# A hybrid Hyena, attention and mixture-of-experts block: inverse square roots by GpSimd as a power, in place of ScalarE's Sqrt and VectorE's reciprocal

## Chip, core and metric

The kernel runs on one core of a Trainium2 chip. The metric is device microseconds of one execution; a kernel is timed several times and the median counts. Before the change it is 795.36 us (three runs, 794.49 to 795.76).

## What is computed

One encoder block over 512 tokens of width 1024, in float32: a Hyena mixer (long convolutions by FFT) and grouped-query attention side by side, a cross-attention over 256 memory rows, and a mixture of 16 experts with two chosen per token. What matters here are its root-mean-square norms, which stand ahead of and behind every stage:

```python
def rms_norm(x, g):
    y = xf * lax.rsqrt(jnp.mean(xf * xf, axis=-1, keepdims=True) + EPS)
    return y * g

h = rms_norm(x, norm_mix)                      # 512 rows of 1024
q = rope_2d(rms_norm(q, q_norm), row, col)     # per head of 64; the same for k
y = concat(group_rms_norm(y_hyena, ...), group_rms_norm(y_attn, ...))   # groups of 64
x = x + y @ w_out
x = x + memory_cross_attn(rms_norm(x, norm_xattn), rms_norm(mem, norm_mem), ...)  # q, k normed per head of 128
x = x + hier_moe(rms_norm(x, norm_moe), ...)
```

## The kernel before

The tokens lie as four tiles of 128 partitions. Every engine has its own instruction stream, written out by hand, and the streams meet in semaphores; an engine works its stream strictly in order, so a wait holds everything behind it. A product with float32 accuracy is made of three TensorE products on split operands: ScalarE makes the high part (`weight_hi`, `split_hi`), VectorE the remainder (`weight_lo`, `split_lo`).

The streams run through these stages: filter spectra of the Hyena mixer with the norms of input and memory (0 to 75 us), its projections and transforms (to 205), the q, k, v projections with rope (to 258), the attention loop of 32 steps (8 heads by 4 tiles, to 345), the output projection (to 390), cross-attention (to 437), the router (to 492), then the experts in a loop of turns of 17.8 us each, bound by TensorE.

In the attention loop step `s` of each engine runs a little ahead of or behind the others. VectorE takes the score maximum of step s+3 (`gqa_max`) and the low part of the transposed probabilities of step s (`gqa_lo`); ScalarE takes the high part of step s and the exponential of step s+2 (`gqa_pt_hi`, `gqa_exp`), and every fourth step copies a finished head out of PSUM (`out_copy`, later `out_rows`); TensorE makes scores, transposes and, every second step, the head's product (`pv`), which needs the low parts of its two steps. GpSimd has little: it squares each head's output (`out_square`, L591), after ScalarE's `out_rows` of that head, in order of the heads, and from the router on it issues the stores, gathers and scatters of rows.

An inverse root takes three steps before: a sum of squares (ScalarE with an accumulator, or VectorE), ScalarE's Sqrt with scale and bias in one instruction (L691, L718, L872, L918, L960), and VectorE's reciprocal (L1188, L1192, L1445, L1458, L1463, L1521, L1581, L1592, L1602, L1658). Sqrt, Sin, Exp and Silu lie in different function tables of ScalarE, and a switch shows in the trace as an `ACT_TABLE_LOAD` on the line of the first function that needs it. Two dummy activations before (L883, L985) bring Exp's table in early, one (L943) brings Sqrt's.

Where the roots stand in order: input rows (L1187) and memory rows (L1191); memory keys (`head_rms(40, ...)`, L825, used at L1580); attention keys (L849, L1444); queries (L882, L1457); Hyena output (`hyena_root`, after step 13 of ScalarE, and `hyena_inverse`, in step 14 of VectorE); attention output in two parts (`out_root`, `out_normed`: six heads at step 29 and 30, two after the loop); the cross-attention norm (L1591), its queries (L984, L1601), and the four tiles ahead of the router (`tile_norm`, `tile_xn`).

Of the kernel before, what the change touches and what calls it, by code (L numbers as in the profile page):

```python
# [130 lines left out]
def build(nc, a, out, xn_dram, y_dram):  # L131
    with ExitStack() as ctx:
# [206 lines left out]
        s_rms = sem("rms_ready")  # L339
        s_ms = sem("head_sums_ready")  # L340
        s_hrms = sem("head_rms_ready")
# [9 lines left out]
        s_hroot = sem("hyena_root_ready")  # L351
        s_hrec = sem("hyena_inverse_ready")
        s_hwide = sem("hyena_inverse_wide")
        s_qinv = sem("qk_norms_ready")
# [222 lines left out]
        def _(pool):  # L577
# [9 lines left out]
            pool.memset(a2[FF:P, 0:1], 0.0).then_inc(s_w3, 1)  # L587

            pool.wait_ge(s_qinv, 1)
# [8 lines left out]
            for h in range(NQ):  # L598
                out_square(h)

            for i in range(TT):
                pool.wait_ge(s_xn, TT + 2 + i + 1)
                pool.dma_start(xn_dram[i * P:(i + 1) * P, :], xn[:, i, :]).then_inc(s_store, 16)
# [64 lines left out]
        def _(act):  # L668
# [16 lines left out]
            def rms(src, first, n, count):  # L685

                for i in range(n):
                    act.activation(fb_flat, src[:, i, :], ACT.Square, accum_out=small[:, first + i:first + i + 1])\
                        .then_inc(s_sq, 1)
                    act.wait_ge(s_sq, count - n + i + 1)  # L690
                act.activation(small[:, 16 + first:16 + first + n], small[:, first:first + n], ACT.Sqrt,  # L691
                               bias=eps, scale=1.0 / D).then_inc(s_rms, 1)
# [21 lines left out]

            def head_rms(first, n, width, count, floor=None):

                act.wait_ge(s_ms, count)
                act.activation(small[:, first:first + n], small[:, first:first + n], ACT.Sqrt, bias=eps if floor is None else floor,  # L718
                               scale=1.0 / width).then_inc(s_hrms, 1)
# [65 lines left out]
            act.activation(a2[FF:P, 1:T], mlp_arg[:, 1:T], ACT.Sin).then_inc(s_sin, 1)  # L785
            act.wait_ge(s_xn, TT + 1)
# [38 lines left out]
            head_rms(40, MT * MH, MHD, 1)  # L825
# [23 lines left out]
            head_rms(230, TT * NKV, HD, 2)  # L849
# [19 lines left out]
            def hyena_root():  # L869
                for n in range(len(HN_STEPS)):  # L870
                    wait_freed(act, ("hn", n))
                act.activation(small[:, 280:312], small[:, 280:312], ACT.Sqrt, bias=eps, scale=1.0 / HD).then_inc(s_hroot, 1)  # L872

            def inverse_wide(c):
                act.wait_ge(s_hrec, 1)
# [6 lines left out]
            head_rms(240, TT * NQ, HD, 3)  # L882
            act.activation(small[:, 398:399], eps, ACT.Exp)  # L883
# [30 lines left out]
            def out_root(lo, hi, count):  # L914

                top = small[:, 340:340 + TT * NQ].rearrange("p (i h) -> p i h", h=NQ)[:, :, lo:hi]
                act.wait_ge(s_ms, count)
                act.activation(top, top, ACT.Sqrt, scale=1.0 / HD).then_inc(s_hrms, 1)  # L918

            for s in range(AHEAD):  # L920
                gqa_exp(s)
            for s in range(NSEQ):
# [13 lines left out]
                if s == HN_STEPS[-1] + 1:  # L936
                    hyena_root()
# [16 lines left out]
            def tile_norm(first, jobkey, count, i):  # L954
# [5 lines left out]
                act.activation(small[:, 16 + first + i:17 + first + i], small[:, first + i:first + i + 1], ACT.Sqrt,  # L960
                               bias=eps, scale=1.0 / D).then_inc(s_rms, 1)
# [22 lines left out]
            head_rms(40, TT * MH, MHD, 6)  # L984
            act.activation(small[:, 398:399], eps, ACT.Exp)  # L985
# [52 lines left out]
            act.activation(rt[:, 204:208], rt[:, 200:204], ACT.Exp).then_inc(s_r4, 1)  # L1038

# [95 lines left out]
        def _(dve):  # L1135
# [37 lines left out]

            range_reduce(0)
# [16 lines left out]
            dve.wait_ge(s_rms, 2)  # L1191
            dve.reciprocal(small[:, 16:18], small[:, 16:18]).then_inc(s_xn, 1)  # L1192
# [251 lines left out]
            dve.wait_ge(s_hrms, 2)  # L1444
            link(dve.reciprocal(small[:, 230:238], small[:, 230:238]))  # L1445
# [63 lines left out]
            def out_roots(lo, hi):  # L1509
# [5 lines left out]
                dve.scalar_tensor_tensor(top, bottom, EPS * HD, top, ALU.mult, ALU.add).then_inc(s_ms, 1)  # L1515

            def out_normed(lo, hi, roots):
# [9 lines left out]
            dve.wait_ge(s_qinv, 1)  # L1527
# [5 lines left out]
            for s in range(NSEQ):  # L1533
# [17 lines left out]
                if s == EARLY_STEP + 1:  # L1551
                    out_normed(0, EARLY, 4)
# [4 lines left out]
            out_normed(EARLY, NQ, 5)  # L1557
# [22 lines left out]
            dve.wait_ge(s_hrms, 1)  # L1580
            link(dve.reciprocal(small[:, 40:48], small[:, 40:48]))  # L1581
# [9 lines left out]
            dve.wait_ge(s_rms, 2 + TT)  # L1591
# [967 lines left out]
```

## Time and profile before

| | |
|---|---|
| median of three runs | 795.36 us |
| lowest, highest | 794.49, 795.76 us |
| span of the profiled execution, first to last instruction | 791.7 us |
| mean granted TensorE clock | 0.987 |
| TensorE busy (matmul) | 747.9 us, 94% |
| VectorE busy | 603.7 us, 76% |
| ScalarE busy | 461.6 us, 58% |
| GpSimd busy | 78.0 us, 10% |

The profile is of one execution; its time outside the span is not on the page, so its span stands beside the runs' median, 3.7 us above it. A busy share is an average over stages with different limits: whether an engine's time counts is read from the chain of work that ended last, which goes back from the last instruction, at each step to what released it.

In the rows below a timeline line gives the start in us, the duration, the engine and line, what was written and read, and in brackets the idle time before it with what ended that; a line of the chain gives start, duration and the work, without what hides behind it. GpSimd is called POOL, TensorE PE, VectorE DVE, ScalarE ACT.

### The profile page before, as it was taken

What the parts mean: (1) busy time and instruction counts of PE and PEld (TensorE: products, weight loads), DVE (VectorE), ACT (ScalarE), POOL (GpSimd) and SP (SyncE); (2) the same over time, 40 slices, a digit from 0 to 9 for tenths busy, and PEclk for the clock granted to TensorE, in tenths of its full rate; (3) what the DMA queues carried; (4) which work ended last, traced back from release to release, by engine and by line L of the source; (5) the groups of instructions that cost most, each with busy time, mean ns of one, the idle gap of its engine ahead of it and who ended that gap; (6) DMA issues with size and microseconds to landing.
All of it is one profiled execution on the core that took longest, in us unless ns stands there. A gap on an engine that the chain in (4) does not pass through costs nothing.

```text
span 791.7 us, 10886 instructions
## 1 busy us (share of the span) xinstructions
PE 747.9 (94%) x3680; PEld 607.8 (77%) x3680; DVE 603.7 (76%) x930; ACT 461.6 (58%) x689; POOL 78.0 (10%) x94
## 2 busy tenths in 40 slices
PE   5899999999999898889999999999999999999994
PEld 3664858788898787678787787888888888888882
DVE  5767482997799877835548568899899999999882
ACT  5952333131233988621559333787888888887782
POOL 0000000000000000000000001122222232222111
PEclk9999999999999999999999998999999999999997
DMA  8830203020120200022130675999999999999741
GB/s 291 298 107 1 84 23 106 27 80 1 38 96 27 78 31 1 2 62 97 54 116 18 246 294 182 420 364 385 379 372 383 373 391 372 369 369 383 306 159 21
DMA packets 28542, 146.53 MB, mean 185 GB/s; under 512 B 4791, under 2 KB 6711, under 8 KB 21976
## 3 DMA queue, kind: packets, MB, share of 16 engines
q1 hardware_dynamic: 23320, 135.53, 45.3%
q0 software_dynamic: 5184, 10.50, 5.0%
q8 instruction: 23, 0.38, 0.2%
q14 instruction: 15, 0.12, 0.0%
HBM read 141.81 MB, written 12.58 MB: 195 GB/s over the span
## 4 chain that ended last, share of the span: by engine, by line
PE 72%; DVE 15%; ACT 6%; DMA 4%; issue 3%; SPq 0%; POOL 0%; DVEq 0%; ACTq 0%; POOLq 0%
PE bank L1992 17%; PE bank L2378 11%; PE bank L2380 10%; PE bank L2379 10%; PE bank L1930 9%; PE bank L1937 3%; DMA slot<-in_w_down 2%; PE bank L2373 2%; PE bank L2004 1%; ACT w_hi L727 1%; PE bank L2292 1%; PE bank L2290 1%; PE bank L2291 1%; DVE w_lo L1165 1%; PE bank L2415 1%
## 5 line engine op out<-in xcount | busy, mean ns | idle before, releaser
L1849 DVE TENSOR_TENSOR e_lo<-slot,e_hi 128x1024 fp32r<-128x1024 f32 x192 | 221.4, 1218 | 9.4 <-ACT e_hi L1045 9.3
L1045 ACT ACTIVATE e_hi<-slot 128x1024 fp32r<-128x1024 f32 x192 | 188.2, 1061 | 7.7 <-DMA slot<-in_w_down 4.9
L1165 DVE TENSOR_TENSOR w_lo<-w_raw,w_hi 128x1024 fp32r<-128x1024 f32 x41 | 49.4, 1222 | 69.8 <-ACT w_hi L727 69.6
L727 ACT ACTIVATE w_hi<-w_raw 128x1024 fp32r<-128x1024 f32 x41 | 42.7, 1057 | 96.9 <-DMA w_raw<-in_w_in 63.2
L2378 PE MATMUL bank<-e_hi,hgT_hi 128*128 128x512 f32 x240 | 95.0, 396 | 0.3 <-DVE hgT_lo L1861 0.3
L2380 PE MATMUL bank<-e_hi,hgT_lo 128*128 128x512 f32 x240 | 93.6, 390 | 0.0
L2379 PE MATMUL bank<-e_lo,hgT_hi 128*128 128x512 f32 x240 | 93.4, 389 | 0.0
L2378 PEld LDWEIGHTS bank<-e_hi,hgT_hi 128*128 128x128 f32 x240 | 45.2, 189 | 9.5 <-DVE hgT_lo L1861 0.7
L2380 PEld LDWEIGHTS bank<-e_hi,hgT_lo 128*128 128x128 f32 x240 | 45.1, 188 | 9.6
L2379 PEld LDWEIGHTS bank<-e_lo,hgT_hi 128*128 128x128 f32 x240 | 45.1, 188 | 8.9
L2378 PE MATMUL bank<-e_hi,gaT_hi 128*128 128x512 f32 x120 | 48.1, 401 | 0.0
L2380 PE MATMUL bank<-e_hi,gaT_lo 128*128 128x512 f32 x120 | 46.9, 391 | 0.0
L2379 PE MATMUL bank<-e_lo,gaT_hi 128*128 128x512 f32 x120 | 46.8, 390 | 0.0
L1992 PE MATMUL bank<-hT_hi,w_hi 128*128 128x512 f32 x96 | 37.9, 395 | 0.0
L1992 PE MATMUL bank<-hT_lo,w_hi 128*128 128x512 f32 x96 | 37.4, 389 | 0.0
L1992 PE MATMUL bank<-hT_hi,w_lo 128*128 128x512 f32 x96 | 37.4, 389 | 0.0
L1992 PE MATMUL bank<-w_hi,hT_hi 128*128 128x512 f32 (+1 forms) x96 | 34.0, 354 | 0.8 <-DVE hT_lo L1171 0.8
L1992 PE MATMUL bank<-w_hi,hT_lo 128*128 128x512 f32 (+1 forms) x96 | 34.0, 354 | 0.0
L1992 PE MATMUL bank<-w_lo,hT_hi 128*128 128x512 f32 (+1 forms) x96 | 34.0, 354 | 0.0
L1063 ACT ACTIVATE hgT_hi<-bank 128x512 fp32r<-128x512 f32 x28 | 15.2, 596 | 31.1 <-PE bank L2373 31.1
L636 POOL DMA_INDIRECT out_dram<-eo,meta_i x16 | 25.4, 1588 | 76.7 <-ACT eo L1080 46.4
L1937 PE MATMUL bank<-ident,pr 128*128 128x128 f32 x160 | 24.8, 277 | 8.1 <-ACT pr L891 6.3
(395 smaller groups left out, 1671.6 us busy)
## 6 DMA issues: line engine op xcount, KB each, us to landing
slot<-in_w_down SPq DMA_DIRECT2D x16, 2048.0 KB, 16.6
slot<-in_w_gate SPq DMA_DIRECT2D x16, 2048.0 KB, 14.6
slot<-in_w_up SPq DMA_DIRECT2D x16, 2048.0 KB, 16.0
w_raw<-in_w_in SPq DMA_DIRECT2D x18, 512.0 KB, 3.5
w_raw<-in_w_out SPq DMA_DIRECT2D x8, 512.0 KB, 3.7
w_raw<-in_w_k_mem SPq DMA_DIRECT2D x4, 512.0 KB, 6.1
x_in<-in_x SPq DMA_DIRECT2D x4, 512.0 KB, 9.2
w_raw<-in_w_v_mem SPq DMA_DIRECT2D x4, 512.0 KB, 6.0
```

Source lines behind the costliest of these rows:

```text
L636: pool.indirect_dma_start(out[0], bass.IndirectOffsetOnAxis(ap=meta_i[:, q, 0:1], axis=0), eo[q][:], None, bounds_check=T - 1, oob_is_err= ...
L727: act.activation(w_hi[ring(m)][:], w_raw[ring(m)][:], ACT.Copy).then_inc(s_wh, 1)
L1045: act.activation(e_hi[buffer(b, j)][:], slot[slot_][:, 1024 * part:1024 * (part + 1)], ACT.Copy).then_inc(s_ehi, 1)
L1165: dve.tensor_tensor(w_lo[slot_][:], w_raw[slot_][:], w_hi[slot_][:].bitcast(F32), ALU.subtract)\
L1849: dve.tensor_tensor(e_lo[slot_][:, at_], slot[slot_][:, at_], e_hi[buffer(b, j)][:].bitcast(F32), ALU.subtract)\
L1930: ins = pe.matmul(dst, l, r, start=(n == 0), stop=(n == len(pairs) - 1))
L1937: ins = pe.transpose(bank(job)[:, n * width:(n + 1) * width], s, ident[:])
L1992: ins = pe.matmul(bank(job)[:, 0:width], left, right, start=(k == 0 and m == 0), stop=(final and m == 2))
L2373: ins = pe.transpose(banks[half][:, k * P:(k + 1) * P], hg[q][:, c:D:KT], ident[:])
L2378: pe.matmul(dst, act_hi, w_hi_, start=first, stop=False)
L2379: pe.matmul(dst, act_hi, w_lo_, start=False, stop=False)
L2380: return pe.matmul(dst, act_lo, w_hi_, start=False, stop=last)
```

## The change

Sqrt leaves ScalarE and reciprocal leaves VectorE. In their place VectorE makes the mean plus epsilon in one step (`tensor_scalar`, multiply and add), counts up `s_mean`, and waits for `s_root`; GpSimd waits for `s_mean`, raises the values to the power -1/2 in place and counts up `s_root`. GpSimd takes the fourteen roots in a fixed order within its own stream. The mean and the wait stand on VectorE where the reciprocal stood (for memory keys: at L1580). Exp's table is brought in by one dummy behind the second Sin, and Silu's by one behind the router's last Exp. The dummies L883, L943 and L985 go.

```diff
@@ gpsimd
-            pool.wait_ge(s_qinv, 1)
+            pool.wait_ge(s_w3, 1)
+            minus_half = small[:, 396:397]
+            link(pool.memset(minus_half, -0.5))
+            roots = [0]
+            def inverse_root(x):
+                roots[0] += 1
+                pool.wait_ge(s_mean, roots[0])
+                pool.tensor_tensor(x, x, minus_half.to_broadcast([P, x.shape[1]]), ALU.pow).then_inc(s_root, 1)
+            def out_inverse_root(lo, hi):
+                roots[0] += 1
+                pool.wait_ge(s_mean, roots[0])
+                x = small[:, 340:340 + TT * NQ].rearrange("p (i h) -> p i h", h=NQ)[:, :, lo:hi]
+                pool.tensor_tensor(x, x, minus_half.unsqueeze(2).to_broadcast([P, TT, hi - lo]), ALU.pow).then_inc(s_root, 1)
+            inverse_root(small[:, 20:24])
+            inverse_root(small[:, 16:18])
+            inverse_root(small[:, 230:238])
+            inverse_root(small[:, 240:272])
             pool.tensor_tensor(ident_pair[:], ident[:, 0:HD], ident[:, HD:P], ALU.add).then_inc(s_pair, 1)
...
             for h in range(NQ):
+                if h == 3:
+                    inverse_root(small[:, 280:312])
                 out_square(h)
-
+                if h == EARLY - 1:
+                    out_inverse_root(0, EARLY)
+            out_inverse_root(EARLY, NQ)
+            inverse_root(small[:, 40:48])
+            inverse_root(small[:, 24:28])
+            inverse_root(small[:, 40:56])
             for i in range(TT):
+                inverse_root(small[:, 28 + i:29 + i])
                 pool.wait_ge(s_xn, TT + 2 + i + 1)
                 pool.dma_start(xn_dram[i * P:(i + 1) * P, :], xn[:, i, :]).then_inc(s_store, 16)
@@ scalar
-                act.activation(small[:, 16 + first:16 + first + n], small[:, first:first + n], ACT.Sqrt,
-                               bias=eps, scale=1.0 / D).then_inc(s_rms, 1)
...
             act.activation(a2[FF:P, 1:T], mlp_arg[:, 1:T], ACT.Sin).then_inc(s_sin, 1)
+            act.activation(small[:, 398:399], eps, ACT.Exp)
...
-            head_rms(240, TT * NQ, HD, 3)
-            act.activation(small[:, 398:399], eps, ACT.Exp)
...
-                if s == HN_STEPS[-1] + 1:
-                    hyena_root()
...
-                if s == EARLY_STEP:
-                    act.activation(small[:, 398:399], eps, ACT.Sqrt)
-                    out_root(0, EARLY, 4)
...
-            out_root(EARLY, NQ, 5)
...
-            head_rms(40, TT * MH, MHD, 6)
-            act.activation(small[:, 398:399], eps, ACT.Exp)
...
             act.activation(rt[:, 204:208], rt[:, 200:204], ACT.Exp).then_inc(s_r4, 1)
+            act.activation(small[:, 398:399], eps, ACT.Silu)
@@ vector
+            roots = [0]
+            def inverse_root(dst, total, width, least=EPS):
+                roots[0] += 1
+                dve.tensor_scalar(dst, total, 1.0 / width, least, ALU.mult, ALU.add).then_inc(s_mean, 1)
+                dve.wait_ge(s_root, roots[0])
...
-            dve.wait_ge(s_rms, 1)
-            link(dve.reciprocal(small[:, 20:24], small[:, 20:24]))
+            dve.wait_ge(s_sq, TT)
+            inverse_root(small[:, 20:24], small[:, 4:8], D)
...
-            dve.wait_ge(s_hrms, 2)
-            link(dve.reciprocal(small[:, 230:238], small[:, 230:238]))
+            inverse_root(small[:, 230:238], small[:, 230:238], HD)
...
-            dve.wait_ge(s_hrms, 3)
-            dve.reciprocal(small[:, 240:272], small[:, 240:272]).then_inc(s_qinv, 1)
+            dve.wait_ge(s_ms, 3)
+            inverse_root(small[:, 240:272], small[:, 240:272], HD)
...
             def hyena_inverse():
-                dve.wait_ge(s_hroot, 1)
-                dve.reciprocal(small[:, 280:312], small[:, 280:312]).then_inc(s_hrec, 1)
+                for n in range(len(HN_STEPS)):
+                    wait_freed(dve, ("hn", n))
+                inverse_root(small[:, 280:312], small[:, 280:312], HD)
...
-                dve.wait_ge(s_hrms, roots)
-                link(dve.reciprocal(top, top))
+                inverse_root(top, top, HD, 0.0)
...
-            dve.wait_ge(s_hrms, 6)
-            link(dve.reciprocal(small[:, 40:56], small[:, 40:56]))
+            dve.wait_ge(s_ms, 4)
+            inverse_root(small[:, 40:56], small[:, 40:56], MHD)
...
             def tile_xn(i):
-                dve.wait_ge(s_rms, 2 + TT + i + 1)
-                link(dve.reciprocal(small[:, 28 + i:29 + i], small[:, 28 + i:29 + i]))
+                dve.wait_ge(s_sq, 6 + TT + i + 1)
+                inverse_root(small[:, 28 + i:29 + i], small[:, 12 + i:13 + i], D)
```

## Rows read from the trace of the kernel before

**Rows 1.** The page, chain that ended last: shares of the span by engine

```profile
PE 72%; DVE 15%; ACT 6%; DMA 4%; issue 3%; SPq 0%; POOL 0%; DVEq 0%; ACTq 0%; POOLq 0%
```

**Rows 2.** Groups by line, ACT: first and last of 13 table loads (us, ns | idle)

```profile
L695 ACT ACT_TABLE_LOAD x1 | 1.3, 1283 | 0.7 <-PEq L2550 0.7
...
L1070 ACT ACT_TABLE_LOAD x1 | 1.3, 1283 | 0.0
```

**Rows 3.** POOL: group by line; timeline at 259 us; one line, ns min/median/max

```profile
L596 POOL TENSOR_TENSOR o_sq<-att 128x256 f32<-128x256 f32 x8 | 5.3, 668 | 81.1 <-ACT att L912 81.1
...
258.99 0.32 POOL L590 TENSOR_TENSOR ident_pair<-ident 128x64 f32<-128x64 f32 x1 [258.16 <-DVE small L1458]
...
L624 POOL COPY gather_i<-rec_i x12: 734/740/1836, 527.6 to 722.8; 128x1 int32 x12
```

**Rows 4.** Timeline, DVE, at the key norm

```profile
244.74 0.20 DVE L1445 RECIPROCAL small<-small 128x8 f32<-128x8 f32 x1
244.97 0.69 DVE L1411 TENSOR_TENSOR qkv<-qkv,small 128x512 f32<-128x512 f32 x1
```

**Rows 5.** Timeline, DVE, at the query norm

```profile
258.55 0.35 DVE L1458 RECIPROCAL small<-small 128x32 f32<-128x32 f32 x1
...
258.94 0.69 DVE L1491 TENSOR_REDUCE small<-bank 128x1 f32<-128x512 f32 x1
```

**Rows 6.** Timeline, 23 to 42 us, then two pieces of the chain

```profile
23.79 0.18 DVE L1188 RECIPROCAL small<-small 128x4 f32<-128x4 f32 x1 [1.16 <-ACT small L691]
...
24.00 2.74 DVE L1190 TENSOR_SCALAR x_in<-x_in,small 128x1024 f32<-128x1024 f32 x4
...
27.08 3.65 PE L1937 MATMUL bank<-ident,x_in 128*128 128x128 f32 x32
...
36.04 1.12 PE L2004 MATMUL bank<-w_sum,a 128*128 128x512 f32 x2 [1.22 <-ACT a L785]
...
41.67 4.87 DVE L1211 TENSOR_TENSOR sum_diff<-bank,decay 128x512 f32<-128x512 f32 x8
...
36.04 7.13 PE bank L2004 x16
...
45.95 3.20 DMA w_raw<-in_w_v_mem
```

**Rows 7.** Timeline, attention loop, around steps 14 and 15

```profile
297.54 0.63 PE L1937 MATMUL bank<-ident,pr 128*128 128x128 f32 x4 [1.86 <-ACT pr L891]
...
299.05 0.39 ACT L912 ACTIVATE att<-bank 128x256 f32<-128x256 f32 x1
...
299.51 0.61 POOL L596 TENSOR_TENSOR o_sq<-att 128x256 f32<-128x256 f32 x1 [10.50 <-ACT att L912]
...
300.16 0.36 PE L1930 MATMUL bank<-pT_hi,v_split 128*128 128x256 f32 x1
```

**Rows 8.** End of the attention loop: timeline, then two pieces of the chain

```profile
337.58 0.68 DVE L1498 TENSOR_TENSOR pT_lo<-bank,pT_hi 128x512 fp32r<-128x512 f32 x1
...
341.27 0.28 PE L1930 MATMUL bank<-pT_hi,v_split 128*128 128x256 f32 x1
...
346.62 0.22 ACT small L918
...
346.86 0.21 DVE small L1521
```

**Rows 9.** Timeline, at the norm of the memory queries

```profile
414.49 0.31 ACT L718 ACTIVATE small<-small 128x16 f32<-128x16 f32 x1
...
415.39 0.67 DVE L1610 TENSOR_REDUCE small<-bank 128x2 f32<-128x512 f32 x1
...
418.01 0.17 DVE L1617 RECIPROCAL small<-small 128x2 f32<-128x2 f32 x1 [0.16 <-ACT pr L995]
```

**Rows 10.** Chain, at the last tile ahead of the router

```profile
468.39 0.29 ACT small L960
```

**Rows 11.** The page, groups of instructions: VectorE's weight splits

```profile
L1165 DVE TENSOR_TENSOR w_lo<-w_raw,w_hi 128x1024 fp32r<-128x1024 f32 x41 | 49.4, 1222 | 69.8 <-ACT w_hi L727 69.6
```

More of the change, by code:

```diff
@@ L338, in build @@
         s_sq = sem("square_done")
-        s_rms = sem("rms_ready")
         s_ms = sem("head_sums_ready")
-        s_hrms = sem("head_rms_ready")
+        s_mean, s_root = sem("mean_square_ready"), sem("inverse_root_ready")
         s_abs = sem("filt_abs_ready")
@@ L350, in build @@
         s_phi = sem("probs_hi_ready")
-        s_hroot = sem("hyena_root_ready")
-        s_hrec = sem("hyena_inverse_ready")
         s_hwide = sem("hyena_inverse_wide")
-        s_qinv = sem("qk_norms_ready")
         s_mkn = sem("mk_normed")
@@ L713, in evac_odd @@
                     free(act.activation(odd[:, c, :], bank(job)[:], ACT.Copy), job)
[L715 to L719, printed above, removed]
             def weight_hi(lo, n):
@@ L824, in _ @@
             evac_odd(("fwd", 1, 1))
-            head_rms(40, MT * MH, MHD, 1)
             weight_hi(23, 3)
@@ L848, in _ @@
             q_split_hi(1, 2)
-            head_rms(230, TT * NKV, HD, 2)
             q_split_hi(2, 3)
@@ L867, in y_square @@
                 act.activation(y_sq[:, c, :], u[:, c, :], ACT.Square).then_inc(s_ysq, 1)
[L869 to L872, printed above, removed]
             def inverse_wide(c):
-                act.wait_ge(s_hrec, 1)
+                act.wait_ge(s_root, 5)
                 act.activation(inv_wide[:, :, c], small[:, 280:312].rearrange("p (t c w) -> p t c w", t=TT, c=CT)[:, :, c, :]
@@ L912, in out_rows @@
                 free(act.activation(out_head(h), bank(job)[:, 0:TT * HD].rearrange("p (i d) -> p i d", i=TT), ACT.Copy), job)
[L914 to L918, printed above, removed]
             for s in range(AHEAD):
@@ L959, in tile_norm @@
                 act.wait_ge(s_sq, count + i + 1)
-                act.activation(small[:, 16 + first + i:17 + first + i], small[:, first + i:first + i + 1], ACT.Sqrt,
-                               bias=eps, scale=1.0 / D).then_inc(s_rms, 1)
             weight_hi(35, 2)
@@ L1186, in _ @@
             range_reduce(1)
-            dve.wait_ge(s_rms, 1)
-            link(dve.reciprocal(small[:, 20:24], small[:, 20:24]))
+            dve.wait_ge(s_sq, TT)
+            inverse_root(small[:, 20:24], small[:, 4:8], D)
             for i in range(TT):
                 dve.tensor_scalar(x_in[:, i, :], x_in[:, i, :], small[:, 20 + i:21 + i], None, ALU.mult).then_inc(s_xn, 1)
-            dve.wait_ge(s_rms, 2)
-            dve.reciprocal(small[:, 16:18], small[:, 16:18]).then_inc(s_xn, 1)
+            dve.wait_ge(s_sq, TT + MT)
+            inverse_root(small[:, 16:18], small[:, 0:2], D)
+            dve.tensor_copy(small[0:1, 397:398], small[0:1, 16:17]).then_inc(s_xn, 1)
             dve.wait_ge(s_arg, 2)
@@ L1514, in out_roots, with out_normed @@
                 link(dve.tensor_tensor(bottom, bottom, bottom, ALU.mult))
-                dve.scalar_tensor_tensor(top, bottom, EPS * HD, top, ALU.mult, ALU.add).then_inc(s_ms, 1)
-            def out_normed(lo, hi, roots):
+                link(dve.scalar_tensor_tensor(top, bottom, EPS * HD, top, ALU.mult, ALU.add))
+            def out_normed(lo, hi):
                 top = heads(340, lo, hi)
-                dve.wait_ge(s_hrms, roots)
-                link(dve.reciprocal(top, top))
+                inverse_root(top, top, HD, 0.0)
                 for h in range(lo, hi, 2):
@@ L1525, in out_normed @@
                         .then_inc(s_att, 1)
-            dve.wait_ge(s_qinv, 1)
             for s in range(AHEAD + 1):
@@ L1551, in _ @@
                 if s == EARLY_STEP + 1:
-                    out_normed(0, EARLY, 4)
+                    out_normed(0, EARLY)
             for h in (NQ - 2, NQ - 1):
@@ L1556, in _ @@
             out_roots(EARLY, NQ)
-            out_normed(EARLY, NQ, 5)
+            out_normed(EARLY, NQ)
             def residual(jobkey, h):
@@ L1578, in mk_normed @@
                 dve.tensor_tensor(x3, x3, row("gmk").unsqueeze(1).to_broadcast([P, MH, MHD]), ALU.mult).then_inc(s_mkn, 1)
-            dve.wait_ge(s_hrms, 1)
-            link(dve.reciprocal(small[:, 40:48], small[:, 40:48]))
+            inverse_root(small[:, 40:48], small[:, 40:48], MHD)
             weight_lo(32, 1)
@@ L1590, in _ @@
                 split_lo(("hT", 1, k), hT_lo[:, k, :], hT_hi[:, k, :], col("norm_xattn", k))
-            dve.wait_ge(s_rms, 2 + TT)
-            dve.reciprocal(small[:, 24:28], small[:, 24:28]).then_inc(s_xn, 1)
+            dve.wait_ge(s_sq, 6 + TT)
+            inverse_root(small[:, 24:28], small[:, 8:12], D)
+            dve.tensor_copy(small[0:1, 397:398], small[0:1, 24:25]).then_inc(s_xn, 1)
             weight_lo(37, 2)
```

## The prediction

> **What bounds the kernel now.** I read the chain of work that ended last first, then the table loads, then the timeline around each of the fourteen roots of the changed order. TensorE carries 72% of the chain, VectorE 15%, ScalarE 6%, GpSimd nothing [rows 1]. So an edit pays only where the chain leaves TensorE, and what matters is how long one inverse root keeps its consumer waiting. The profiled span is 791.7 us and the median of the three runs 795.36; I take the 3.7 us outside the span as unchanged, and add the change of the span to 795.36.
>
> **What leaves ScalarE.** 13 table loads of 1283 ns [rows 2]. In the changed order Sin, Exp and Silu remain behind the first load, so four loads stay and nine go: 9 x 1.28 = 11.5 us of ScalarE, with seventeen Sqrt of 0.2 to 0.3 us. Most of it stands beside TensorE work and is worth nothing; the exceptions are below.
>
> **What a power costs.** No row shows one. Write its time as a + b x n for n columns. GpSimd's 128x256 product takes 0.668 us and its 128x64 sum 0.32 [rows 3], so a plain pass has b = 1.8 ns and a = 0.2 us. That is the lower bound: a power does not cost less than a product on the same engine. For the upper side only rows of other engines help. VectorE's reciprocal goes from 0.20 us at 8 columns to 0.35 at 32 [rows 4, 5], 6 ns a column, where a plain pass over 512 columns takes 0.69 [rows 5], about 1.1 ns with its fixed 0.15 taken off: a harder function costs about six plain passes. A power is a logarithm, a product and an exponential; as three to four such functions it is some 22 passes, 22 x 1.8 = 40 ns a column. I take b = 40 ns, an estimate, nearer the reciprocal's rows than the product's; I let it range from 1.8 to 165 ns (four times my value). Then 1, 8, 16, 24 and 32 columns take 0.24, 0.52, 0.84, 1.16 and 1.48 us. The Trainium skill, GPSIMD Engine Reference, § Performance pitfalls for Q7 kernels, prices a chain of dependent fp32 steps at 4 cycles an element (at the page's 1.2 GHz); if a power were 25 such steps, that is 83 ns a column, an estimate from the page, and the sum below would be +8.1 us, not +3.9. No row here shows it.
>
> Around each power stand a mean step on VectorE (0.18, as a small reciprocal) and two hand-overs: 0.09 to GpSimd (258.90 to 258.99) [rows 3, 5] and 0.03 back; 0.30 us in all. VectorE waits idle meanwhile, so its whole queue stands behind each root.
>
> **Part by part.** (P8 is the power over 8 columns, and so on; plus is a loss.)
>
> *Start.* VectorE is free at 23.79 - 1.16 = 22.63 and then waits for Sqrt and its load. Now: 22.63 + 0.30 + P4 + 2.74 of scaling = 25.7 + P4, while TensorE takes the first transpose at 27.08 [rows 6]. P4 = 0.36 hides; over 1.35 us it would not. With no Sqrt between the two Sin, the load ahead of the second one goes. TensorE waited 1.22 for that Sin [rows 6]. But Exp's new load, with its dummy, stands right behind it, so ScalarE's next work comes 0.1 to 0.2 later, not earlier, and the filter products leave their banks through VectorE, in order behind weights that ScalarE splits: first bank free at 41.67 + 0.61 + 0.15 = 42.4, and the next product group, which entered at 36.04 + 7.13 = 43.17, enters at about 42.6 [rows 6]. That group releases the 3.20 us weight load at 45.95 which the chain waits for [rows 6]. Gain 0.55 (from 0 to 1.22).
>
> *Key norm.* VectorE is the chain here: reciprocal at 244.74, next step at 244.97 [rows 4]. 0.23 becomes 0.30 + P8: P8 + 0.07.
>
> *Query norm.* The reciprocal starts at 258.55 and the first maximum at 258.94 [rows 5]: 0.39 becomes 0.30 + P32: P32 - 0.09. The Exp load that goes here stood beside it.
>
> *Hyena norm (step 14).* Two loads and a Sqrt go from ScalarE, 2.9 us, and TensorE's wait of 1.86 for the exponential goes with them [rows 7]. But GpSimd's queue holds the root behind the square of head 2, and that stands behind ScalarE's copy of head 2, 299.05 [rows 7]. With TensorE 1.86 earlier the copy runs at 297.19 to 297.58, the square (0.61) ends at 298.26 and VectorE wakes at 298.3 + P32. Behind its wait are the next maximum and split (0.69 + 0.68, [rows 5, 8]), and TensorE needs that split, then 0.45 of transposes, for the head's product: 300.15 + P32 and some hand-overs, where before it stood at 300.16 [rows 7]. The stall is not removed, it moves from ScalarE to VectorE: P32 + 0.1.
>
> *First six heads' output norm.* P24 stands beside TensorE's output products: VectorE ended its last split at 337.58 + 0.68 = 338.26 and TensorE takes it at 341.27 [rows 8]. 3.0 us of cover: nothing; without it P24 + 0.1.
>
> *Last two heads.* Sqrt at 346.62 to reciprocal's end at 347.07 [rows 8], 0.45, becomes 0.30 + P8: P8 - 0.15.
>
> *Memory queries.* Sqrt starts at 414.49 and the first maximum at 415.39 [rows 9]; the two small steps between them that stay took 0.31. Now 414.49 + 0.30 + P16 + 0.31 = 415.10 + P16: 0.29 earlier less P16. ScalarE's exponentials no longer stand behind a load, so the 0.16 for which VectorE waited on them at 418.01 [rows 9] goes as well: P16 - 0.45.
>
> *Last tile ahead of the router.* ScalarE's 0.29 of Sqrt [rows 10] and 0.19 of reciprocal go, 0.30 + P1 comes: P1 - 0.15. The other three tiles have TensorE work in front.
>
> *At nothing:* memory keys, cross-attention norm and mean steps there: VectorE idles 69.8 us ahead of its 41 weight splits, nearly all for ScalarE's halves and so for loads [rows 11], and a root of 0.7 to 0.8 us lies in such a gap; if not, it costs its own length. On GpSimd's queue the four stores of normalised rows come between the last roots, but each waits for the row that its root produces. Silu's load moves ahead of expert weights for which there is time.
>
> **Sum.** Fixed: -0.55 + 0.07 - 0.09 + 0.10 - 0.15 - 0.45 - 0.15 = -1.22. Powers on the chain: two of 32 columns, two of 8, one of 16, one of 1: six times 0.2 = 1.2, and 97 columns. So the change is 0.0 us + 97 x b. At 40 ns +3.9: **799.2 us**. With b between 16 and 90 ns, 797 to 804.
>
> **Rivals.**
> 1. *Not slower: the power is as cheap as a product.* For it: products and sums are all that the rows show of the engine's arithmetic; against: the reciprocal's slope. At 1.8 ns, 97 x 1.8 = +0.2: 795.5. It decides from b = 1.6 / 97 = 16 ns a column down.
> 2. *The power is far dearer*, say a scalar routine. For it: GpSimd took 0.74 us for an index copy of a single column [rows 3], over three times the plain price. At 200 ns, +19.4: 814.8; roots at the start and under the output products would then begin to show too.
> 3. *The hyena root isn't held up* by the square of head 2 (head 2 copied in time). Then that step gains 1.86, not loses P32 + 0.1: -3.4, 795.7; with cheap powers too, 793.2, the only clear gain I can build.
> 4. *The first power starts late, as code that has to be fetched.* GpSimd's index copy took 1.84 us once and 0.74 in the middle [rows 3], 1.1 more, which the 1.0 us left at the start nearly hides; a fetch like the 3.20 us load [rows 6] would cost 2.2 and the 0.55: 802.0. The Trainium skill, GPSIMD Engine Reference, § Instruction dispatch, says that the first call to freshly loaded code pays about 6 us that no instruction shows; by it the sum would be +9.5 us. No row shows such a first call.
> 5. *The loads don't go:* absolute values ran only under Sin's table before. If Exp's lacks them, loads come back in the filter stage, 2.6 us: 801.8.
>
> **How the numbers follow.** Forecast (b 16 to 90) 0.44; cheap 0.27; dear 0.16; root not held up 0.07; late first call 0.04; loads stay 0.02. Most of the cheap case, half of the third rival and a little of the forecast's edge lie within 0.2% (1.6 us, about what a measurement of this kernel can tell from none): 0.30. Faster takes the rest of the third rival and an underrated gain at the start: 0.09. Slower 0.61. The range leaves out 0.08 below 794.6 and 0.12 above 811.5 (b over 165 ns).
>
> **What would show it.** Four table loads; VectorE's gap ahead of the key scaling, the first maximum, the split of step 15 and the last heads' product, each as long as its power and 0.1; at step 14 GpSimd running head 2's square right before the root, about 3 us after VectorE's mean step; the filter products starting about 1.2 us earlier. I am wrong in size if the 32-column power isn't near 1.5 us, and in kind if TensorE doesn't wait for VectorE at step 15.

## The result: 2.6% slower, and the profile after

The changed kernel takes 816.08 us (median of 4 runs, 814.09 to 816.78) against 795.4 for the kernel before on the same chip: ratio 1.0261, 95% interval 1.0236 to 1.0286, or +20.7 us. The forecast was 799.2, with a range up to 811.5. The sign was right and the size was not.

The profiled execution took 815.84 us with a span of 814.0. In every run of this study the time lies 1.8 to 1.9 us above the span. So the profiled execution of before, span 791.7, took about 793.6, and the 3.7 us that the prediction read as "outside the span" were half spread between executions. A comparison of the two traces (+22.3 us of span) is therefore 1.6 us larger than that of the medians.

The chain of the changed kernel on its page, shares by engine:

```profile
PE 69%; DVE 13%; ACT 6%; issue 5%; DMA 4%; POOL 3%; SPq 0%; DVEq 0%; ACTq 0%; POOLq 0%
```

Its groups of instructions by line and shape: GpSimd's powers, then all of ScalarE's table loads (us busy, mean ns of one, idle before):

```profile
L593 POOL TENSOR_TENSOR small<-small 128x32 f32<-128x32 f32 x2 | 10.8, 5418 | 13.9 <-DVE small L1172 13.9
...
L600 POOL TENSOR_TENSOR small<-small 128x24 f32<-128x24 f32 x1 | 4.2, 4157 | 7.2 <-DVE small L1172 7.2
L593 POOL TENSOR_TENSOR small<-small 128x8 f32<-128x8 f32 x2 | 3.3, 1636 | 234.7 <-DVE small L1172 234.7
L593 POOL TENSOR_TENSOR small<-small 128x16 f32<-128x16 f32 x1 | 2.9, 2894 | 15.8 <-DVE small L1172 15.8
...
L593 POOL TENSOR_TENSOR small<-small 128x1 f32<-128x1 f32 x4 | 2.2, 552 | 46.0 <-DVE small L1172 46.0
L593 POOL TENSOR_TENSOR small<-small 128x4 f32<-128x4 f32 x2 | 2.1, 1031 | 55.3 <-DVE small L1172 55.3
...
L717 ACT ACT_TABLE_LOAD x1 | 1.3, 1283 | 0.7 <-PEq L2550 0.7
L703 ACT ACT_TABLE_LOAD x1 | 1.3, 1283 | 0.0
L802 ACT ACT_TABLE_LOAD x1 | 1.3, 1283 | 0.0
L1031 ACT ACT_TABLE_LOAD x1 | 1.3, 1283 | 0.0
```

Nine loads are gone, as forecast [rows 2]. GpSimd, which had no share of the chain [rows 1], now has 3%, and "issue" (time in which the engine waited for nothing that the profile shows) went from 3 to 5%. A power takes (5.418 - 1.636) / 24 = 0.158 us a column and 1.636 - 8 x 0.158 = 0.37 us besides; 1, 4 and 16 columns lie on the same line. The forecast took 0.040 a column.

Who waited for it: waits of VectorE in the changed kernel (us in total, times, longest), then of TensorE:

```profile
DVE small L1493 <- POOL small L593: 14.0, 2, 8.5
...
DVE att L1525 <- POOL small L600: 6.0, 2, 4.3
...
DVE small L1603 <- POOL small L593: 3.0, 1, 3.0
DVE xn L1659 <- POOL small L593: 2.7, 4, 0.7
...
DVE qkv L1413 <- POOL small L593: 1.8, 1, 1.8
```

```profile
PE bank L1937 <- ACT pr L899: 9.2, 6, 6.9
PE bank L1937 <- DVE pT_lo L1500: 7.1, 1, 7.1
...
PE bank L1992 <- DVE yT_lo L1164: 3.5, 2, 2.7
```

VectorE stands idle 14.0 us before two of its row maxima (L1493): 5.5 at the query norm and 8.5 at step 14. Two lines of TensorE repeat these two waits one engine later: 6.9 for the first exponential, 7.1 for the split that VectorE does after the wait of step 14. The 2.7 is a third stall, behind the root of the last two heads. The 8.5 is longer than the power, which takes 5.42. GpSimd's timeline shows why:

```profile
297.19 0.61 POOL L612 TENSOR_TENSOR o_sq<-att 128x256 f32<-128x256 f32 x1 [9.16 <-ACT att L920]
306.26 0.61 POOL L612 TENSOR_TENSOR o_sq<-att 128x256 f32<-128x256 f32 x1 [8.46 <-ACT att L920]
306.83 5.42 POOL L593 TENSOR_TENSOR small<-small 128x32 f32<-128x32 f32 x1
```

VectorE posted its mean at 303.63 + 0.17 = 303.80. GpSimd sat in front of the square of head 2, waiting for ScalarE's copy of that head, until 306.26, and began the power at 306.83, 3.0 us late. That is the forecast's picture of step 14, with a power of 5.42 in place of 1.48.

A second effect stood in no term of the sum. Stretches of the changed kernel (us, then busy time of PE, PEld, DVE, ACT and POOL, granted clock of TensorE, DMA share, GB/s):

```profile
262.00:266.00 4.00, 0.00 (x0) 0.00 (x0) 0.25 (x1) 0.00 (x0) 3.99 (x2) 0.87 0.00 0
266.00:270.00 4.00, 2.41 (x10) 2.22 (x11) 3.12 (x8) 2.92 (x7) 0.00 (x0) 0.50 0.00 0
270.00:274.00 4.00, 4.00 (x26) 3.82 (x26) 2.72 (x7) 2.28 (x7) 0.00 (x0) 0.78 0.00 0
...
310.00:314.00 4.00, 0.17 (x1) 0.17 (x2) 1.68 (x4) 0.79 (x2) 2.25 (x1) 0.50 0.00 0
314.00:318.00 4.00, 4.00 (x18) 3.70 (x19) 1.59 (x4) 1.39 (x4) 0.00 (x0) 0.50 0.00 0
318.00:322.00 4.00, 3.53 (x22) 2.71 (x21) 3.51 (x9) 4.00 (x10) 0.00 (x0) 0.80 0.01 2
...
366.00:370.00 4.00, 4.00 (x13) 3.19 (x14) 2.20 (x3) 0.00 (x0) 0.00 (x0) 0.67 0.00 0
```

The same two stretches of the kernel before, at its own times:

```profile
266.00:270.00 4.00, 4.00 (x32) 3.57 (x31) 3.93 (x9) 3.83 (x8) 0.00 (x0) 1.00 0.00 0
...
310.00:314.00 4.00, 3.47 (x25) 2.60 (x24) 3.13 (x7) 4.00 (x10) 0.00 (x0) 1.00 0.00 0
```

TensorE does nothing from 262 to 266 while GpSimd is busy for 3.99 us; then it starts again with a granted clock of 0.50, the lower of its two levels (1.2 of 2.4 GHz), and is back at 1.00 only after 274. The same follows the stall of step 14 and the shorter one of 2.7 us behind the last heads (0.67 at 366 to 370). In the kernel before the clock is 1.00 in all of it. So these stalls are paid twice, once while TensorE waits and once while it works slowly; what the second costs is measured by e2_busy below.

### The profile page after: what moved, and what is told of

It reads as the page before. It is cut to its first block, busy times and chain, and to the rows that moved or that the text cites. A ratio compares the mean times of both kernels' runs of the same rounds, so it can differ in the third digit from the quotient of the medians.

```text
span 814.0 us, 10885 instructions
## 1 busy us (share of the span) xinstructions
PE 755.4 (93%) x3680; PEld 614.3 (75%) x3680; DVE 604.1 (74%) x932; ACT 446.1 (55%) x662; POOL 103.5 (13%) x109
## 4 chain that ended last, share of the span: by engine, by line
PE 69%; DVE 13%; ACT 6%; issue 5%; DMA 4%; POOL 3%; SPq 0%; DVEq 0%; ACTq 0%; POOLq 0%
PE bank L1992 17%; PE bank L2378 10%; PE bank L2380 10%; PE bank L2379 10%; PE bank L1930 9%; PE bank L1937 2%; POOL small L593 2%; DMA slot<-in_w_down 2%; PE bank L2373 2%; PE bank L2317 1%; ACT pr L987 1%; DVE w_lo L1158 1%; PE bank L2292 1%; PE bank L2291 1%; PE bank L2290 1%
## 5 line engine op out<-in xcount | busy, mean ns | idle before, releaser
L593 POOL TENSOR_TENSOR small<-small 128x1 f32<-128x1 f32 (+5 forms) x12 | 22.0, 1832 | 368.6 <-DVE small L1172 368.6
L1493 DVE TENSOR_REDUCE small<-bank 128x1 f32<-128x512 f32 x32 | 21.9, 685 | 21.7 <-POOL small L593 14.0
L899 ACT ACTIVATE pr<-bank,small 128x512 f32<-128x512 f32 x32 | 25.3, 791 | 18.1 <-DVE small L1494 18.1
```

Source lines behind the costliest of these rows:

```text
L593: pool.tensor_tensor(x, x, minus_half.to_broadcast([P, x.shape[1]]), ALU.pow).then_inc(s_root, 1)
```

## Where the 22 us of the trace went

Start of the same instruction in each trace, as its distance from the kernel before (us, from the timelines). The first row is the kernel before's own time. The short names are those of the experiments below.

| kernel | copy of head 0 | head 2 | head 3 | head 7 | fourth split of the attention half (yT, high part) | first copy of memory probabilities | high part of the gathered rows | end of span |
|---|---|---|---|---|---|---|---|---|
| before, at | 278.16 | 299.05 | 308.18 | 344.64 | 354.82 | 420.04 | 492.76 | 791.7 |
| changed | +8.8 | +6.8 | +15.3 | +15.9 | +18.9 | +21.1 | +22.1 | +22.3 |
| line | -1.0 | -1.5 | +1.4 | +1.8 | +1.8 | +1.5 | +3.2 | +1.2 |
| busy | +6.1 | +5.7 | +13.0 | +13.6 | +15.0 | +17.2 | +20.2 | +20.4 |
| order | +7.8 | +5.8 | +11.4 | +12.0 | +15.0 | +17.4 | +20.4 | +20.3 |
| ahead | -1.0 | -3.0 | -3.0 | -2.5 | -1.7 | -2.6 | -1.3 | -2.6 |

Between head 0 and head 2 the changed kernel gains 2.04 us, the wait for the two table loads at step 13 to 14 that the prediction put at 1.86. From head 2 to head 3 it loses 8.55. Ahead of head 0 stand 1.69 at the key norm and 5.32 at the query norm (VectorE's key scaling 244.97 to 246.46, from 0.20 early to 1.49 late; first maximum 258.94 to 265.75), and 2.0 of low clock.

Two low-clock stretches stand in every trace, around the end of the router (in the kernel before 0.64 at 472 to 476 and 0.50 at 488 to 492). Others come and go from trace to trace: 0.66 at 776 to 780 in the kernel before, 0.75 and 0.82 between heads 0 and 1 in the line kernel, 0.57 at 290 to 294 in the busy one. Such a stretch shifts what follows by 1 to 2 us (between heads 0 and 1 the line kernel loses 1.56, the busy one 1.59). So a step of one ledger is good to about that, and the medians decide.

## The experiments

The kernel before was timed again beside them: 795.23 us (23 runs) on the chip of e1_line, e2_busy, e3_order and e6_ahead, 795.70 (26 runs) on that of the four others with several runs. So a difference of medians between the two chips is good to about half a microsecond, and the ratios are given with it.

**Take the length of the power away (e1_line).** VectorE's mean step carries a slope and an offset, GpSimd multiplies by one:

```diff
-pool.tensor_tensor(x, x, minus_half..., ALU.pow).then_inc(s_root, 1)
+pool.tensor_tensor(x, x, one..., ALU.mult).then_inc(s_root, 1)
-dve.tensor_scalar(dst, total, 1.0 / width, least, ALU.mult, ALU.add)
+dve.tensor_scalar(dst, total, slope / width, offset, ALU.mult, ALU.add)
```

> Each inverse root is replaced by a straight line in the mean square (the slope and the offset stand in the mean step on VectorE, GpSimd multiplies by 1.0), so every instruction, wait and queue stays and only the power's length goes; the output isn't the reference's. Theory A (the length of the powers on the chain is the loss, with the lower clock that follows the long idle stretches): the sum of the prediction with plain products, 795.4 - 1.2 + 6 x 0.25, so 795 to 797. Rival B (the hand-overs, the added waits and GpSimd's queue order cost time by themselves): 803 or more.

Measured: 793.53 us (10 runs), ratio to before 0.9977, interval 0.9961 to 0.9992. Theory A, though 1.5 us below the 795 to 797 that it gave; rival B falls. The power's length and what hangs on it are 816.1 - 793.5 = 22.6 us, more than the whole loss. GpSimd in that kernel:

```profile
257.72 0.24 POOL L593 TENSOR_TENSOR small<-small 128x32 f32<-128x32 f32 x1 [13.87 <-DVE small L1177]
...
298.06 0.61 POOL L612 TENSOR_TENSOR o_sq<-att 128x256 f32<-128x256 f32 x1 [8.45 <-ACT att L920]
298.63 0.24 POOL L593 TENSOR_TENSOR small<-small 128x32 f32<-128x32 f32 x1
```

A product over 32 columns takes 0.24 us, about the prediction's lower bound (0.2 + 32 x 0.0018 = 0.26). But even it starts only at 298.63, behind the square of head 2, with VectorE's mean posted at 295.44 + 0.17 = 295.61: the queue's 3.0 us are there without the power.

**Keep TensorE busy through the stalls (e2_busy).** Products of constants into banks that are free there:

```diff
-FILL = [3, 3, 2, 2] + [1] * 6
+FILL = [32, 3, 2, 2] + [1] * 6
+                    if s == 15:
+                        constant_products(("hr", 0), 30)
                     qT_job(2 + QT_STEPS.index(s))
+            constant_products(("yT", CT - 1), 11)
             chunk_jobs("wo0", yT_hi, yT_lo, part=slice(2, 3), ...)
```

> The changed kernel with products of constants put into TensorE's three long idle stretches: 29 more ahead of the first attention transpose, 30 at step 15, 11 ahead of the third part of the output product; each took about 0.14 to 0.22 us in the changed kernel's trace. Theory A (after the query stretch, the Hyena stretch and the one under the last heads the granted clock stood at 0.50 to 0.80 and the stage ledger shows 2.0 + 1.4 + 1.6 us for it): 3 to 5 us less, 811 to 813, with the granted clock at 1.00 in these stretches. Rival C (the stages behind the stretches are paced by ScalarE and VectorE, a slower TensorE costs nothing): 815.5 to 816.5.

Measured: 812.33 us (4 runs), 3.75 less, ratio to before 1.0215 (1.0190 to 1.0240). Theory A; rival C falls. Two of the stretches in this kernel:

```profile
262.00:266.00 4.00, 4.00 (x38) 4.00 (x37) 0.88 (x3) 0.00 (x0) 3.33 (x2) 1.00 0.00 0
266.00:270.00 4.00, 3.61 (x29) 3.26 (x28) 3.82 (x9) 3.79 (x9) 0.00 (x0) 1.00 0.00 0
...
310.00:314.00 4.00, 3.59 (x32) 3.40 (x32) 2.72 (x6) 0.87 (x2) 1.18 (x1) 1.00 0.00 0
```

The clock stays at 1.00, and the ledger loses 2.0 us of its steps up to head 0, 1.2 from head 2 to head 3 and 1.6 up to the fourth split: 4.8, of which this execution gives some 3 back in low stretches elsewhere. Nothing but useless work was added, and the kernel is faster: the low clock is a cost of its own, 3.75 us by the medians and 4.8 by the ledger.

**Move one line in GpSimd's queue (e3_order, and e7_line_order on the straight-line kernel).**

```diff
-                if h == 3:
+                if h == 2:
                     inverse_root(small[:, 280:312])
                 out_square(h)
```

> One line moved: GpSimd takes the Hyena root ahead of the square of head 2, not behind it. VectorE posts the mean at 303.80 and the power starts at 306.83 in the changed kernel's trace. Theory A (step 14's stall is the power plus GpSimd's queue): the power starts 2.9 us earlier and the time falls by 2.5 to 3.5 us, to 812.5 to 813.5. Rival D (the square of head 2 held up nothing, or is then late itself, so that VectorE's head sums wait): 815.5 to 816.5.

> The straight-line kernel (793.5 us) with the Hyena root taken by GpSimd ahead of the square of head 2; output not the reference's, as there. Theory A2 (at step 14 two terms stand side by side, the power's length and GpSimd's queue: in the straight-line kernel VectorE posts the mean some 3 us before GpSimd reaches it, although the product takes 0.24 us): 2.0 to 2.9 us less, 790.6 to 791.6, and the copy of head 3 comes 2 to 3 us earlier against the copy of head 2. Rival F (with a short operation the queue is hidden behind TensorE's work): 793 to 794.

Measured: 811.32 us (4 runs) for the changed kernel, 4.8 less, and 790.38 (5 runs, ratio 0.9936) for the straight-line one, 3.2 less (3.3 by the two ratios). GpSimd with the real power, then with the product:

```profile
302.93 5.43 POOL L593 TENSOR_TENSOR small<-small 128x32 f32<-128x32 f32 x1 [6.08 <-DVE small L1172]
308.33 0.61 POOL L612 TENSOR_TENSOR o_sq<-att 128x256 f32<-128x256 f32 x1
```

```profile
294.16 0.24 POOL L593 TENSOR_TENSOR small<-small 128x32 f32<-128x32 f32 x1 [6.08 <-DVE small L1177]
296.54 0.61 POOL L612 TENSOR_TENSOR o_sq<-att 128x256 f32<-128x256 f32 x1 [2.13 <-ACT att L920]
```

The root now starts when VectorE posts the mean. From head 2 to head 3 the ledger loses 5.6 instead of 8.55 with the power, and nothing (-2.98 to -2.97) instead of 2.8 with the product. So at step 14 two terms stand side by side, 3 us of queue and 5.4 of power; rivals D and F fall. The median of e3_order fell by 1.3 us more than I expected; its trace shows the 2.95 at step 14, and another 0.95 up to head 0, ahead of the edit; so the rest is left to the spread of four runs.

**Do the terms add? (e8_two_lines)** The product in place of the two 32-column powers only:

```diff
+op, by = (ALU.mult, ones_col) if roots[0] in (4, 5) else (ALU.pow, minus_half)
-pool.tensor_tensor(x, x, minus_half..., ALU.pow).then_inc(s_root, 1)
+pool.tensor_tensor(x, x, by..., op).then_inc(s_root, 1)
```

> The changed kernel with straight lines in place of the two 32-column powers only (query norm and Hyena norm); the other twelve powers stay; output not the reference's. Theory A (the stage ledger adds up): 816.1 less 2 x 5.17 of power, less 2.0 and 1 to 1.5 of low clock behind the two stretches: 802 to 803. Rival G (the terms don't add: what one stretch costs is taken back in the next): 805 or more, or below 799.

Measured: 800.11 us (10 runs), ratio 1.0058 (1.0038 to 1.0078). This is neither: 1.9 below A's range and 1.1 above the 799 under which G would have held. The twelve other powers cost 800.1 - 793.5 = 6.6 us (6.4 by the ratios). By their own lengths it is 2 x 1.44 (8 columns, twice), 2.68 (16), 0.37 (1) and 0.6 where the 24-column power outlasts its cover: 6.5. The two large ones then cost 16.0, of which 10.3 is length. The traces of the two kernels place 3.8 more as low clock: 2.0 up to head 0; at step 14 only 0.2 (a loss of 8.55 against 3.16, less 5.18 of length), since e8_two_lines too was granted 0.57 there (300 to 304), behind a TensorE stall of 1.93 us that the queue left; and 1.6 behind the last heads, where A expected nothing. There TensorE's stall is 2.68 us in both kernels. The changed kernel's ends so, and its clock then falls to the 0.67 shown above:

```profile
365.89 0.47 PE L1992 MATMUL bank<-w_hi,yT_hi 128*128 128x512 f32 x1 [2.68 <-DVE yT_lo L1164]
```

In e8_two_lines it ends at 353.10, and the clock stays at 1.00:

```profile
352.00:356.00 4.00, 2.90 (x13) 2.45 (x14) 3.40 (x5) 0.38 (x1) 0.00 (x0) 1.00 0.05 20
356.00:360.00 4.00, 3.93 (x20) 2.93 (x18) 0.01 (x1) 0.73 (x2) 0.00 (x0) 1.00 0.07 8
```

So the terms don't add one by one: in these two traces, one execution each, what a stall costs afterwards isn't fixed by its own length. Some 2 us are in no ledger, and I can't say where they stand.

**Put the roots ahead of their use (e6_ahead).** The same powers, posted when their sums are ready and waited for where they are read; the edits at the query norm and the Hyena norm:

```diff
+            mean(small[:, 240:272], small[:, 240:272], HD)
             for c in range(CT):
                 skipped(1, c)
-            inverse_root(small[:, 240:272], small[:, 240:272], HD)
+            dve.wait_ge(s_root, 4)          # heads 0 and 1; the others at head 2
...
+            out_square(0)
+            hyena_root(0)                   # 16 columns, when their sums leave the bank
+            out_square(1)
+            hyena_root(1)
+            out_square(2)
```

> The same powers, but none is waited for at once: the key mean is posted right after its sum, 4 us ahead of its use; the query mean ahead of the four skip products, in two powers (heads 0 and 1, then the rest, waited for at head 2); the Hyena mean in two halves at steps 9 and 13, waited for by ScalarE alone; output norm in four powers, heads 0 to 3, 4 and 5, 6, 7; the memory queries tile by tile, with the factor folded into the mean step. Theory A (a power costs what VectorE waits for it, nothing else): left on the chain are about 1.0 us for the last head, 1.0 for the memory queries and 0.55 for the last tile, against 0.45, 0.9 and 0.48 that go; the Sqrt loads at step 14 go with 1.86: 793 to 795. Rival E (GpSimd at work beside VectorE slows VectorE, or the added small steps on VectorE cost as much as they hide): 797 to 803.

Measured: 791.25 us (12 runs), ratio to before 0.9964 (0.9950 to 0.9979): faster than both kernels, and 1.8 us below the range that A gave. Theory A; rival E falls. It still spends 5.75 us in the query powers and 2.9 in each half of the Hyena root, but VectorE's waits for GpSimd's roots are down to these, and GpSimd's share of the chain is 0% again:

```profile
DVE xn L1666 <- POOL small L591: 2.7, 4, 0.7
...
DVE att L1533 <- POOL small L591: 2.3, 2, 1.2
...
DVE x_in L1200 <- POOL small L591: 1.2, 1, 1.2
DVE small L1601 <- POOL small L591: 1.1, 1, 1.1
...
DVE small L1204 <- POOL small L591: 0.8, 1, 0.8
```

The same powers, as long as before, now cost next to nothing: what cost in the changed kernel was that VectorE stood still for each with its whole queue behind.

**Put the two table loads back at step 14 (e9_loads).** In the kernel with the roots ahead:

```diff
+                if s == HN_STEPS[-1] + 1:
+                    act.activation(small[:, 394:395], eps, ACT.Sqrt)
+                    act.activation(small[:, 393:394], eps, ACT.Exp)
```

> The kernel with the roots posted ahead (791.25 us), and on ScalarE after the exponential of step 13 a dummy Sqrt and a dummy Exp, so that the two table loads that the change took from step 14 stand there again. Theory H (most of what the removed loads are worth on the chain is this one wait of 1.86 us of TensorE): 1.6 to 2.2 us more, 792.9 to 793.5, and the copy of head 2 about 2 us later. Rival I (the gain of the kernel with roots ahead comes from elsewhere): 791 to 791.8.

Measured: 795.48 us (12 runs), ratio to before 0.9994 (0.9978 to 1.0011): the gain of the kernel with the roots ahead is gone. In its trace ScalarE's two loads stand at step 14 again, and TensorE waits behind them for 1.32 us, where it waited 1.86 before [rows 7]:

```profile
291.73 1.28 ACT L953 ACT_TABLE_LOAD   x1
...
293.23 1.28 ACT L954 ACT_TABLE_LOAD   x1
...
296.12 0.63 PE L1947 MATMUL bank<-ident,pr 128*128 128x128 f32 x4 [1.32 <-ACT pr L913]
```

The copy of head 2 comes 1.57 us later and stays so. Theory H for the place; the median lies 2 us above its range (0.2 by the two ratios). The size is open between this 1.6 and the 4.2 of the medians (2.4 by the two ratios): the profiled execution, 793.07, is one of the two fastest of the twelve, with a mean granted clock of 0.989 where the slower ten have 0.979 to 0.986. That the stall brings a low-clock stretch in most executions fits this, but no trace shows one there.

**Move Exp's load at the start (e10_late_exp).**

```diff
-            act.activation(small[:, 398:399], eps, ACT.Exp)    # behind the second Sin
...
             weight_hi(4, 3)
+            act.activation(small[:, 398:399], eps, ACT.Exp)
             abs_pair(0, 0)
```

> The kernel with the roots posted ahead, and Exp's load with its dummy moved from right behind the second Sin to behind the next four weight halves, where ScalarE waits for VectorE for 2.9 us. Theory J (the prediction's step: Exp's load at that place eats what the removed Sin load gives): the copies of the memory keys come 1.2 to 1.5 us earlier, the copies of the memory values about as much, and the time falls by 0.4 to 1.3, to 790.0 to 790.9. Rival K (the weight transfers bound this stretch): the memory values come at the same time, 791 to 791.8.

Measured: 791.92 us (8 runs), ratio 0.9949 (0.9929 to 0.9969): not to be told from e6_ahead (791.25 on the other chip; by the ratios 1.2 us less, with intervals that overlap). In the trace the memory keys' copies come 1.2 us earlier (36.46 to 35.26), the memory values' copies 0.6 (54.85 to 54.27), the copy of head 0 0.7. So the load did eat what the removed one gave at that place, half of it is lost again to a weight transfer that ScalarE waits 0.65 us for, and what is left is below what these medians resolve. Neither theory is settled by the time.

**Is it columns or elements? (e11_lanes)** Two more powers on GpSimd, off the chain:

```diff
+pool.tensor_tensor(small[0:16, 381:389], small[0:16, 240:248], half[0:16], ALU.pow)
+pool.tensor_tensor(small[0:1, 389:393], small[0:1, 240:244], half[0:1], ALU.pow)
```

> The kernel with the roots posted ahead, and two more powers on GpSimd after the query roots, where it is idle: 8 columns over 16 partitions, and 4 columns over 1 partition (over all 128 partitions 8 columns took 1.64 us and 4 took 1.01). Theory L (the price is one of columns, the partitions run side by side): 1.6 and 1.0 us. Rival M (the engine works through the elements, partitions included): well under 0.8 us for the first and 0.4 or less for the second. In either case the kernel's time stays at 791 to 793, as the two stand off the chain.

```profile
254.97 5.75 POOL L591 TENSOR_TENSOR small<-small 128x8 f32<-128x8 f32 x2 [13.46 <-DVE small L1184]
...
260.97 1.64 POOL L621 TENSOR_TENSOR small<-small 16x8 f32<-16x8 f32 x1
262.58 1.00 POOL L622 TENSOR_TENSOR small<-small 1x4 f32<-1x4 f32 x1
```

16 x 8 takes 1.64 us like 128 x 8, and 1 x 4 takes 1.00 like 128 x 4. Theory L: columns have a price, partitions none. The kernel took 792.1 us in its one run.

## Why the prediction was wrong

*What bounds the kernel, and where the roots stand.* Right: the key and query norms, step 14, the last heads, the memory queries and the last tile are where the time went; memory keys and cross-attention norm, put at nothing, show no step in the ledger.

*What a power costs.* This is the step that failed: I took b = 40 ns a column, from the slope of VectorE's reciprocal times three to four, and named 165 ns as the end; it is 158, with a = 0.37 us, not 0.2. With these two numbers the prediction's own sum is -1.22 + 6 x 0.37 + 97 x 0.158 = +16.3 us, or 811.7. So 12.5 of the 16.9 us by which I was wrong are this one term. I weighed two sources with one inference each (a plain pass on the same engine, a hard function on another) and let their middle stand, with nothing in the trace to pick it. The bound at four times my value was nearly the truth, and the chance I gave to a far dearer power, 0.16, was too small. That rival 2's 814.8 lies so near the measured 816.1 is in part luck: its 200 ns are 42 too many, and make up for most of the clock term that it lacks. By the Trainium skill, GPSIMD Engine Reference, § Performance pitfalls for Q7 kernels, at 4 cycles a step and the page's 1.2 GHz, 158 ns would be some 47 dependent steps, an estimate; the page gives no number of steps for a power, and no run here counts them. The 25 steps, or 83 ns, that I set there were short as well.

*The stalls are paid twice.* This term the sum put at nothing, without a word: what TensorE loses after it has stood still, here twice for 7 us and once for 2.7. The trace shows the clock at 0.50 behind each of the two long stalls; e2_busy takes the low clock away and gains 3.75, the ledger 4.8. That is the size of the other 4.4 us of the miss. With a power of 1.48 the two long stalls would have been some 3 us, not 7. The term would not have been nothing even so: in e1_line, where TensorE stood still for 1.93 us at step 14, the clock was 0.63 behind it (300 to 304).

*Key norm, query norm.* P8 + 0.07 is 1.71 with the measured power, the ledger shows 1.69. P32 - 0.09 is 5.33, the ledger shows 5.32.

*Step 14.* The mechanism was right in every part: loads gone (2.04 for 1.86), GpSimd at the square of head 2 right before root 5, TensorE waiting for VectorE's split at step 15. P32 + 0.1 is 5.5 with the measured power; the ledger has 8.55 - 2.04 = 6.5, and the 1.2 of low clock that e2_busy takes away here are about the difference. Rival 3 (by its own numbers 799.2 - 3.4 = 795.8, not 795.7), the root not held up, falls; e3_order and e7_line_order show what it would have been worth, 3 us.

*First six heads.* Put at nothing, as long as the power stays within its cover. The power isn't 1.16 but 4.16, and 0.6 us show through (heads 6 to 7, +15.28 to +15.86). With the 3.0 us of cover that I read it would have been 4.16 + 0.1 - 3.0 = 1.3, so the cover was some 3.7.

*Last heads, memory queries.* P8 - 0.15 is 1.49, the ledger shows 1.43 at the third part of the output product (348.60 to 365.89, against +15.86 at head 7). P16 - 0.45 is 2.44, the ledger shows 2.1.

*Last tile.* P1 - 0.15 was wrong in kind by a little. I took ScalarE's Sqrt off the path, but it stood beside VectorE's split of the tile. VectorE at that place, before and after:

```profile
469.25 0.69 DVE L1653 TENSOR_TENSOR hT_lo<-bank,hT_hi 128x512 fp32r<-128x512 f32 x1 [0.62 <-ACT hT_hi L1022]
469.86 0.15 DVE L1658 RECIPROCAL small<-small 128x1 f32<-128x1 f32 x1
470.05 1.28 DVE L1659 SCALAR_TENSOR_TENSOR xn<-x,small,g_moe 128x1024 f32<-128x1024 f32 x1
```

```profile
490.93 0.14 DVE L1172 TENSOR_SCALAR small<-small 128x1 f32<-128x1 f32 x1
491.75 1.28 DVE L1659 SCALAR_TENSOR_TENSOR xn<-x,small,g_moe 128x1024 f32<-128x1024 f32 x1 [0.67 <-POOL small L593]
```

From 0.19 to 0.82, +0.63, where P1 - 0.15 gives 0.40 (the prediction's own terms, 0.30 - 0.29 - 0.19, make P1 - 0.18).

*Start.* Forecast -0.55. The filter products start 0.5 us earlier (36.04 to 35.55), not 1.2, and the memory values' copies lie between 0.44 earlier and 0.57 later than before in the nine traces of changed kernels. Nothing that counts; the sign is not settled.

*Rivals 4 and 5.* The first power, over 4 columns, took 1.05 us and a later one 1.01, and it began at 22.91, 0.16 us after VectorE had its mean (22.60 + 0.15): no late first call. The Trainium skill, GPSIMD Engine Reference, § Instruction dispatch, puts about 6 us on the first call of freshly loaded code, which no instruction shows; this trace has no such gap. Whether the power is code of that kind no run shows. The loads went as the change says.

*Left open.* With the straight line the kernel is 1.7 us faster than before, where the prediction's sum with plain products gives +0.1. Its trace shows 0.8 of these 1.8 us ahead of head 0 and 0.2 at step 14's loads; the rest has no place. So the fixed part of the sum was some 1.7 us too dear, and some 2 us of the two 32-column powers (e8_two_lines) have no place in the ledger; in the total the two hide each other.

## What to carry to other kernels

When an operation has no row, price it between its bounds by what a wrong choice would cost, and let the range reach the dear end: here the sum was 97 times an unknown. Before moving a step to another engine, look for the earliest point at which its input is complete: posted there and waited for at its use, some 30 us of powers cost next to nothing and the freed table loads show as a gain; waited for at once, 28 us of them cost 22. Look at what stands ahead of it in the new engine's queue, and allow, behind every stall of TensorE, for what it may lose afterwards (here 1.2 to 2.0 us behind three of them, by the ledger).

## What the runs showed of the hardware that I had not expected

- GpSimd's fp32 power takes 0.37 us and 0.158 us a column, whatever the number of partitions (128 x 8 and 16 x 8: 1.64 us each); its product over 32 columns takes 0.24. A root over 128 x 32 values is over 22 times as long as the product.
- Beside some work of VectorE a power is longer: the 8-column one took 2.01 us beside VectorE's products of two operands in SBUF (key norm, e6_ahead), 1.64 with VectorE waiting; VectorE's own instructions kept their 0.69. Beside the skip products, which read one operand from a bank, 8 and 24 columns took 5.75 together, no more than their 1.64 + 4.16 alone. The Trainium skill, GPSIMD Engine Reference, § Key points, says that the two engines share their SBUF interfaces and contend when VectorE reads two SBUF inputs; the two rows agree.
- Useless products during a stall make the kernel faster: 3.75 us for 70 of them.
- Behind the same TensorE stall of 2.68 us, at the same place, the granted clock fell to 0.67 in the trace of the changed kernel and stayed at 1.00 in that of e8_two_lines.
